# Six pairs of MLP up blocks in place of five as seven products of sums, and a new item order within a pair

## The reference

```python
x = x + rms_norm(y, norm_mix_post[l])
h = rms_norm(x, norm_mlp_pre[l])
u = jnp.square(jax.nn.relu(jnp.einsum('bsd,df->bsf', h, w_up[l])))      # 2048 -> 8192
x = x + rms_norm(jnp.einsum('bsf,fd->bsd', u, w_down[l]), norm_mlp_post[l])
```

## Time and profile before

| what | value |
|---|---|
| median of 3 runs | 1916.93 us (1916.89 to 1916.99) |
| the profiled execution | 1916.62 us, span 1914.7 us |
| TensorE | 1898.4 us busy, 99% of the span, 8662 matmuls |
| VectorE | 1426.9 us busy, 75% |
| ScalarE | 1016.4 us busy, 53% |
| granted TensorE clock, mean | 0.998 |
| transfers | 419.67 MB, mean 219 GB/s |

### The profile page before, as it was taken

The page is one execution under the profiler, slowest core; times in us unless marked ns, Lnnn a source line. Parts: engine busy times, 40 slices in busy tenths (PEclk is TensorE's granted clock), DMA queues, the critical chain, the costliest instruction groups (busy, mean ns, idle before and its releaser), DMA issues.

```text
span 1914.7 us, 21994 instructions
## 1 busy us (share of the span) xinstructions
PE 1898.4 (99%) x8662; PEld 1580.7 (83%) x8662; DVE 1426.9 (75%) x1400; ACT 1016.4 (53%) x979; POOL 19.8 (1%) x31
## 2 busy tenths in 40 slices
PE   9999999999999999999999999999999999999998
PEld 7888888888888878888788888887899888888886
DVE  7847648854766699888978988898587869776665
ACT  7334445555435456555565565565555456544553
POOL 0000000000000000000000000000000000000000
PEclk9999999999999999999999999999999999999999
DMA  8865976765767457777587473565577444446752
GB/s 324 266 213 180 273 249 224 220 250 197 258 204 286 173 174 270 272 234 272 177 283 266 176 266 134 201 221 219 199 222 245 173 176 157 163 176 235 233 197 110
DMA packets 259911, 419.67 MB, mean 219 GB/s; under 512 B 192860, under 2 KB 199264, under 8 KB 219360
## 3 DMA queue, kind: packets, MB, share of 16 engines
q1 hardware_dynamic: 258792, 416.69, 63.6%
q10 hardware_dynamic: 1016, 1.59, 0.2%
HBM read 390.96 MB, written 27.27 MB: 218 GB/s over the span
## 4 chain that ended last, share of the span: by engine, by line
PE 86%; DVE 9%; ACT 3%; issue 2%; DMA 1%; SPq 0%; POOL 0%; DVEq 0%; POOLq 0%; ACTq 0%
PE acc L1992 79%; PE mis L1992 6%; DVE lo L1280 4%; DVE m L1260 2%; ACT hi L833 1%; ACT hi L830 1%; DVE at L1326 1%; DVE xs L1260 1%; PE mis L1995 1%; DMA m<-in_w_down 0%; ACT m L811 0%; DMA raw<-in_w_down 0%; DVE sm L1260 0%; DMA raw<-in_w_in 0%; DVE xs L1268 0%
## 5 line engine op out<-in xcount | busy, mean ns | idle before, releaser
L1992 PE MATMUL acc<-hi,at 128*128 128x512 f32 (+1 forms) x4944 | 1532.8, 388 | 3.9 <-DVE lo L1280 2.6
L1992 PEld LDWEIGHTS acc<-hi,at 128*128 128x128 f32 x4944 | 925.0, 188 | 190.9 <-DVE lo L1280 4.1
L1992 PE MATMUL acc<-lo,at 128*128 128x512 f32 (+1 forms) x2472 | 954.8, 387 | 0.0
L1280 DVE TENSOR_TENSOR lo<-raw,hi 128x2048 fp32r<-128x2048 f32 (+1 forms) x303 | 681.1, 2257 | 243.4 <-ACT hi L833 237.1
L833 ACT ACTIVATE hi<-raw 128x2048 fp32r<-128x2048 f32 (+1 forms) x288 | 539.9, 1886 | 240.4 <-PE acc L1992 134.6
L1992 PEld LDWEIGHTS acc<-lo,at 128*128 128x128 f32 x2472 | 464.2, 188 | 90.8 <-DVE lo L1290 0.5
L811 ACT ACTIVATE m<-acc,st 128x512 f32<-128x512 f32 (+2 forms) x84 | 55.9, 665 | 116.1 <-PE acc L1992 114.9
L1260 DVE TENSOR_TENSOR m<-m 128x256 f32<-128x256 f32 (+1 forms) x147 | 76.4, 520 | 28.6 <-ACT m L811 24.3
L1280 DVE TENSOR_TENSOR lo<-xs,hi 128x2048 fp32r<-128x2048 f32 x35 | 80.1, 2288 | 18.9 <-ACT hi L830 15.4
L811 ACT ACTIVATE m<-m 128x512 f32<-128x512 f32 (+4 forms) x71 | 58.2, 819 | 59.9 <-DVE m L1260 37.7
L830 ACT ACTIVATE hi<-xs 128x2048 fp32r<-128x2048 f32 x26 | 49.8, 1915 | 58.2 <-DVE xs L1260 50.9
(11 more groups left out here) (169 smaller groups left out, 1054.0 us busy)
## 6 DMA issues: line engine op xcount, KB each, us to landing
raw<-in_w_in SPq DMA_DIRECT2D x133, 1024.0 KB, 5.2
raw<-in_w_up SPq DMA_DIRECT2D x54, 1024.0 KB, 6.2
raw<-in_w_down SPq DMA_DIRECT2D x44, 1024.0 KB, 6.9
raw<-in_w_out SPq DMA_DIRECT2D x32, 1024.0 KB, 5.3
m<-turned SPq DMA_DIRECT2D x144, 128.0 KB, 4.2
raw<-in_w_pg SPq DMA_DIRECT2D x16, 1024.0 KB, 5.6
turned<-m SPq DMA_DIRECT2D x28, 512.0 KB, 4.4
xs<-in_w_down SPq DMA_DIRECT2D x12, 1024.0 KB, 6.8
```

Of the source, the lines that this page charges most:

```text
L1280: e.tensor_tensor(lo, raw, hi.bitcast(F32), ALU.subtract).then_inc(s_lo.on("lo", n))
L1992: return e.matmul(o, a, b, start=start, stop=stop)
```

## The change

`UP_PAIRS` goes from five pairs to six: blocks 2-3, 4-5, 6-7, then plain block 8, then 9-10, 11-12, 13-14, then plain block 15. Within a pair the order of items is new. The rest follows from these two: where blocks are taken and turned, which buffers the transfers of the later `ut` blocks wait for, and where an accumulation is closed (3a now stands between S5 and S6).

```diff
-UP_PAIRS = (2, 5, 8, 11, 13)
-UP_ORDER = "S0 S1 2b S2 2a S3 S4 3b 3a S5 S6".split()
+UP_PAIRS = (2, 4, 6, 9, 11, 13)
+UP_ORDER = "S0 2b S1 2a S2 S3 3b S4 S5 3a S6".split()
...
-                chunks.append((weights(p, k, c), 512, b0 + 1 - c, 4 * len(ids), 8 if c else 12, "r1", 4 * k))
+                chunks.append((weights(p, k, c), 512, b0 + 1 - c, 4 * len(ids), 8, "r1", 4 * k))
...
-        up_evac = {seven_at[p, 0, 5] if c else seven_at[p, 0, 6] + 1: number["up", j] for j, (p, c) in up_seven.items()}
+        up_evac = {seven_at[p, 0, 6] + (-1 if c else 1): number["up", j] for j, (p, c) in up_seven.items()}
...
-                         seven_at[up_seven[j][0], 0, 5] + (3 if up_seven[j][1] else 5) for j in range(16)})
+                         seven_at[up_seven[j][0], 0, 6] + (1 if up_seven[j][1] else 3) for j in range(16)})
...
-            heads_at["ut", j] = issue_behind(seven_at[UP_LAST, 0, 6] - LEAD + 1)
+            heads_at["ut", j] = issue_behind(seven_at[UP_LAST - 1, 0, 6] - LEAD + 1)
...
-                    sp.wait_ge(s_lo, "lo", seven_at[UP_LAST - 1, 0, 6])
+                    sp.wait_ge(s_lo, "lo", seven_at[UP_LAST, 0, 6])
...
-                            sp.wait_ge(s_lo, "lo", seven_at[UP_LAST, 0, 6])
+                            sp.wait_ge(s_lo, "lo", seven_at[UP_LAST - 1, 0, 6])
...
-                    r = mm(o, c, hv[:, j, :], False, k + j == nk - 1)
+                    r = mm(o, c, hv[:, j, :], False, k + j == nk - 1 and (t, blocks[b][3][-1]) != (1, n + 1))
...
-                opens, closes = q in (0, 1, 2, 4) and g == 0, q in (0, 1, 2, 4) and g == last or p > 1 and q > 4
+                opens, closes = q in (0, 1, 2, 4) and g == 0, q in (0, 1, 2, 4) and g == last or p > 1 and q == 6
```

## The result

The changed kernel takes 1925.46 us (median of 5 runs, 1924.46 to 1926.11), the kernel before 1916.93: a ratio of 1.0041 with an interval of 1.0030 to 1.0053. It is **slower by 8.5 us**, where 2.7 us were forecast, and above the range. The profiled execution took 1926.11 us.

The account below looks back on a forecast made before the run. PE's matmul count was taken as the bound, DVE as second limit. New stalls and restarts of 9.2 us, less old stalls of 3.8 and removed matmuls of 2.7, gave +2.7 us: 1919.6 us, range 1915.4 to 1924.2.

Parts of the forecast that it names:

- PE bounds: Whole kernel: TensorE busy 99% of the span; in the up stage DVE's `low` releases its stalls, 3.8 us together.
- DVE per pair: Up stage, new order: 42.5 us of DVE work per pair against 40.8 on PE, rounding waits near 0.3 us.
- Added: DVE work for the one more pair: `low`, sums, `mixed` and two takings, some 21 us.
- First run: Pairs 2-3, 4-5, 6-7: DVE late by 3.7 us at item 36, 3b of the third pair.
- second run: Pairs 9-10, 11-12, 13-14: DVE late by 2.0 us at 3b of the last pair.
- ACT at four places: Where two pairs meet, DVE waits for ACT's Relu, Square and rounding of S3: 0.3 us each, 1.2 us in all.
- The y buffer: T1 of the third pair: DVE waits 0 to 3.1 us for y from SP's queue, taken as 1.5 us.
- The upper bound: Top of the forecast range for the whole kernel, 1924.2 us, set at the middle of rival c.
- rival c: SP's queue bounds: each us of 3a's raw landing above 7.1 costs one in each of four pairs; 1922.8 us, chance 0.32.
- A stall outside the up stage: Sign that the prediction is wrong: a PE stall beyond the up stage, for which it saw no cause; no size given.
- The sum: Whole kernel: new stalls and restarts 9.2 us, less old stalls 3.8 and removed matmuls 2.7, gives +2.7 us.

Follow-up runs that it names:

- shorter turns: Changed kernel with HEADS3 moved behind y, where DVE also transposes only 32 of 512 columns of each pair block's half: 1918.61 us, ratio 1.0004.
- the two with five pairs: New item order with the five pairs of the kernel before, run twice against that kernel: 1915.95 us (0.9992), then 1915.22 us (0.9988).

## Why the prediction was wrong, point by point

- **PE bounds, DVE's `low` is the second limit:** right. 8650 matmuls; every stall in the stage is released by a `low`.
- **DVE per pair, 42.5 us with 0.3 of waits:** right. (Under "Added", 3 `low` and 4 sums are 7 operations and not 6.5; the "some 21 us" holds all the same, with 20.6 measured.) The cycle shown is 42.93 us with 0.2 of waits, and the PE stalls within one, 0.44 + 1.42 and two restarts, are the 2.1 us by which it is above 40.8. The figure of the Trainium skill (VectorE: DVE Perf Modes, TRN2 errata), 2.29 us for each operation, would have been some 0.4 us more for a pair than 2.26; the trace has starts 2.20 apart where neighbours don't depend on each other.
- **First run, 3.7 without y and ACT; second run, 2.0; ACT at four places, 1.2:** together 6.9 and 0.8 of restarts; 7.4 measured with HEADS3 behind y. The split was a little off: ACT's share was nothing, since DVE came later than its rounding; with shorter turns the wait appears, 1.2 us in each following pair. Without restarts, the first run of pairs lost 3.9 us there and the second 2.7.
- **The y buffer, 1.5 us (0 to 3.1): this is the step that failed.** It measured 5.97 and 5.13. Its frame held: T3 ended 0.3 us from the time worked out, counted from the first S0, and so did the moment at which DVE wanted y. The transfers did not. Two prices were taken from a place where a HEADS stood behind one raw load: HEADS2 at 5.1 (measured 7.0 and 8.0), HEADS3 at 4.8 with its gap (6.2 and 5.6). Raw and x took 2.4 and 1.3 of issue in the two profiles, where the sum had 1.3. So y was issued at 770.3 to 770.8, on the scale of the kernel before, instead of 766.1, and landed 6.2 to 6.5 later. The prediction listed this queue and saw that x now stood in it; it did not ask what x ahead of HEADS does to HEADS. HEADS3 moved behind y shows the price, 6.2 us of median, and HEADS2 moved ahead of x shows the cause, 5.1 us for 7.0 and 8.0. The upper bound carried the same prices, so the range was too low as well.
- **Half clock behind a long stall:** not in the sum. In the changed kernel it adds 1.5 us of slow matmuls, and nearly all of it comes back in the next stall, that of the third pair's 3b, which is gone.
- **Raw landings above 7.1 (rival c):** not so as a rule. The two rows of the transfers, as the earlier trace rows, over 690 to 960 us:

```profile
raw<-in_w_up SPq DMA_DIRECT2D x38, 1024.0 KB, 6.5
xs<-in_w_up SPq DMA_DIRECT2D x16, 512.0 KB, 7.2
```

ACT waits for raw loads for 18.3 us there, where 9.3 stood before, and DVE 4.2 us for the roundings behind them; PE loses nothing by it in this trace. Rival (c) had the right queue and the right sign, but put its price on the raw of 3a, in four pairs; what came late was y, once.
- **A stall outside the up stage, named as a sign of being wrong:** there is one, the wait for DVE at 1321.99. Between the matmuls that the kernel before starts at 1093 and 1364 us, all ten profiles with six pairs take 0.5 to 1.5 us longer than it, the two with five pairs 0.2 to 0.3. Why it is longer stays open.
- **The sum:** with 5.97 in place of 1.5 and the half clock, less what was over in the other terms, it is +6.8 in place of +2.7 (+6.6 with the old stalls counted alike). The medians differ by 8.5. The stretch above has 0.9 of what is between; about 1 us is not settled. With HEADS3 behind y, 7.4 - 4.0 - 2.7 = +0.7, 1.2 behind the up stage and 0.3 at its end make 2.2, and 1.9 was measured. With five pairs, 1.2 - 4.0 + 0.3 = -2.5, and -1.4 and -1.9 were measured.

## What to carry to other kernels

A sixth pair saves 2.7 us of TensorE, but each pair directly behind another costs 0.9 to 2.1 us of stalls, as DVE has 42.9 us of work for 40.8, and the sixth makes three more such places (four in place of one): the gain of one engine must be set against the next one's slack at that place. In an in-order DMA queue, price a scattered transfer by what is still in flight ahead of it, not by its length elsewhere, and put what an engine waits for first; here one such transfer moved behind y was worth 6 us. Before counting on an idle engine, look whether it shares ports with the busy one.

## What the runs showed of the hardware

- Four scattered transfers of 128 KB held SP's queue between 2.7 us (nothing in flight ahead of them) and 12.1 us (4 MB).
- After PE stalls of 3.74 us (HEADS2 behind raw), 5.52, 6.37 and 7.80 us the granted clock was 0.50 for some 6, 10, 7 and 13 matmuls, 0.427 us apart; after stalls up to 2.1 us it never was. With T3 on GpSimd it was also seen after stalls of 3.6 and 2.8 us and after one of 2.5 us, but not after another of 2.5.
- In 3 of 13 profiled executions, of three different kernels, the first 12 us have 36 or 37 matmuls for 42 to 45, up to 2.0 us.
- A 128x2048 float32 sum took 4.6 us on GpSimd, and a DVE operation with both inputs in SBUF, begun beside it, took about as much longer as GpSimd still ran.
